# Where an expert tile's gated rows are transposed: between the two chunks of the running down product

## The reference

```
combine = jnp.sum(jax.nn.one_hot(expert_id, N_EXPERTS, dtype=f32) * w2[..., None], axis=1)
out = jnp.zeros_like(t)
for e in range(N_EXPERTS):                     # 16 experts, each token goes to 2
    hid = jax.nn.silu(t @ w_gate[e]) * (t @ w_up[e])     # 1024 -> 512
    out = out + combine[:, e:e + 1] * (hid @ w_down[e])  # 512 -> 1024
```

## Time and profile before

| | |
|---|---|
| time, median of 3 runs | 1016.9 us (1015.62 to 1018.69) |
| profiled execution | 1016.17 us, span 1014.4 us |
| PE busy | 963.5 us, 95% of the span |
| DVE busy | 670.7 us, 66% |
| ACT busy | 549.9 us, 54% |
| POOL busy | 267.7 us, 26% |
| mean granted TensorE clock | 0.988 |

### The profile page before, as it was taken

One profiled execution on the slowest core, in us unless ns is written; L12 is line 12 of the kernel. 1 busy time (PEld: TensorE's weight loads), 2 busy tenths in 40 slices (PEclk: granted clock), 3 DMA queues, 4 the chain that ended last, 5 costly groups with the idle time before them and its releaser, 6 DMA issues.

```text
span 1014.4 us, 16745 instructions
## 1 busy us (share of the span) xinstructions
PE 963.5 (95%) x5977; PEld 848.4 (84%) x5977; DVE 670.7 (66%) x860; ACT 549.9 (54%) x613; POOL 267.7 (26%) x184
## 2 busy tenths in 40 slices
PE   5999899999999999899999999989899999999986
PEld 3999789889978988799999986777688888888874
DVE  5496769669857875611111115389989899898966
ACT  5645544825544473233333214357687777878743
POOL 1014213313413231244333433015101101010161
PEclk9999999999999999999999999989899999999998
DMA  9552141304223311232332279269999999999987
GB/s 283 193 181 63 48 125 46 107 21 145 63 67 104 82 42 42 64 84 83 92 95 83 83 196 360 104 210 336 404 400 415 412 415 410 413 412 414 382 212 177
DMA packets 147847, 199.46 MB, mean 197 GB/s; under 512 B 14568, under 2 KB 91774, under 8 KB 147300
## 3 DMA queue, kind: packets, MB, share of 16 engines
q1 hardware_dynamic: 139866, 171.83, 48.9%
q0 software_dynamic: 4656, 16.21, 5.2%
q10 hardware_dynamic: 3290, 10.97, 2.8%
HBM read 176.06 MB, written 22.92 MB: 196 GB/s over the span
## 4 chain that ended last, share of the span: by engine, by line
PE 75%; DVE 14%; issue 5%; ACT 3%; DMA 1%; DVEq 1%; POOL 0%; SPq 0%; ACTq 0%
PE PJ L481 62%; DVE MEM_R L2121 3%; DVE MEM L1850 2%; PE NM L1396 2%; PE PJ L1332 2%; DVE MEM L1953 1%; PE MS L1365 1%; PE MS L1618 1%; PE NM L1553 1%; DMA MEM<-in_x_prompt_dram 1%; PE MS L1388 1%; PE PJ L1431 1%; PE NM L1654 1%; DVE M_Y L1960 1%; DMA RAW<-in_w_out_dram 1%
## 5 line engine op out<-in xcount | busy, mean ns | idle before, releaser
L481 PE MATMUL PJ<-MEM_R 128*128 128x272 f32 (+2 forms) x5016 | 799.5, 320 | 10.7 <-DVE MEM_R L2037 2.8
L481 PEld LDWEIGHTS PJ<-MEM_R 128*128 128x128 f32 x5016 | 718.2, 189 | 73.8 <-issue 12.4
L726 POOL TENSOR_TENSOR MEM_R<-RAW,MEM_R 128x1024 fp32r<-128x1024 f32 x72 | 177.6, 2474 | 343.6 <-ACT MEM_R L875 343.6
L2121 DVE TENSOR_TENSOR MEM_R<-CHUNK,MEM_R 128x2048 fp32r<-128x2048 f32 x100 | 225.5, 2294 | 16.9 <-ACT MEM_R L1138 15.7
L1138 ACT CAST MEM_R<-CHUNK 128x2048 fp32r<-128x2048 f32 x100 | 189.4, 1912 | 15.6 <-PE PJ L481 9.0
L875 ACT CAST MEM_R<-RAW 128x1024 fp32r<-128x1024 f32 x81 | 84.2, 1048 | 122.1 <-DMA RAW<-in_w_pb_dram 39.6
L2023 DVE TENSOR_TENSOR MERGED<-PJ,MEM 128x544 f32<-128x544 f32 x14 | 10.1, 725 | 132.4 <-PE PJ L481 132.4
L806 POOL COPY MEM<-MEM 128x1 uint32 (+1 forms) x16 | 22.5, 1407 | 227.0 <-PE MS L1618 227.0
L1850 DVE SCALAR_TENSOR_TENSOR MEM<-MEM 128x548 f32<-128x548 f32 x72 | 58.9, 818 | 8.5 <-DVE MEM L1848 0.9
L1156 ACT CAST MEM_R<-MS 128x1024 fp32r<-128x1024 f32 x17 | 17.3, 1017 | 27.5 <-PE MS L1618 27.5
L932 ACT COPY MEM<-PJ 128x272 f32<-128x272 f32 x24 | 9.0, 376 | 39.9 <-PE PJ L481 39.9
(11 more groups left out here) (344 smaller groups left out, 939.9 us busy)
## 6 DMA issues: line engine op xcount, KB each, us to landing
CHUNK<-in_w_gate_dram SPq DMA_DIRECT2D x34, 1024.0 KB, 7.5
CHUNK<-in_w_up_dram SPq DMA_DIRECT2D x34, 1024.0 KB, 9.2
CHUNK<-in_w_down_dram SPq DMA_DIRECT2D x34, 1024.0 KB, 8.3
RAW<-in_w_in_dram SPq DMA_DIRECT2D x56, 512.0 KB, 3.7
expert_rows<-MEM ACTq DMA_DIRECT2D x15, 512.0 KB, 6.0
expert_rows<-MEM SPq DMA_DIRECT2D x10, 512.0 KB
RAW<-in_w_pa_dram SPq DMA_DIRECT2D x8, 512.0 KB, 3.6
RAW<-in_w_pb_dram SPq DMA_DIRECT2D x8, 512.0 KB, 3.7
```

Source lines behind the costliest of these rows:

```text
L481: ins = pe.matmul(out, w(a), x(b), start=first and n == 0, stop=last and n == 2)
L726: tt(lo, raw[slot], hi.bitcast(F32), ALU.subtract).then_inc(lo_done, 1)
L2121: tt(moe_hl[c][1], moe_raw[c], moe_hl[c][0].bitcast(F32), ALU.subtract).then_inc(chunk_lo[c], 1)
```

## The change

Inside the loop and in the written-out stage ahead of it (tile 1) `down` is called in two halves, with `turn_hidden` between them. ACT's, DVE's, POOL's and SP's instructions stay as they are, and so do all matmuls and their operands.

```
             pe.wait_ge(extra_ready, 1)
-            down(1)
+            down(1, (4,))
             turn_hidden(1)
+            down(1, (5,))
             last = pe.value_load(last_i[0:1, 0:1], min_val=NE - 1, max_val=TILES - 1)
             with pe.Fori(2, TILES) as i:
                 with pe.If(i < last):
                     gate_up(i)
                     turn_rows(i + 2)
-                    down(i)
+                    down(i, (4,))
                     turn_hidden(i)
+                    down(i, (5,))
```

## The result

The changed kernel takes 1025.42 us in the median (1024.33 to 1026.72) beside 1017.8 of the kernel before: a ratio of 1.0084, with a 95% interval of 1.0062 to 1.0105. That is 7.6 us slower where 5.1 were forecast. The time lies in the stated range and the direction is right; the size is half again what was forecast. Two later comparisons of the same kernel gave 1.0061 (1.0040 to 1.0081) and 1.0078 (1.0048 to 1.0107).

A forecast was written before the change was run, and what follows sets the result against it. PE's own work was taken to bound the loop, 17.80 us a pass without waits. Terms: 3.2 (tiles 1 and 2) + 2.3 (tiles 3 to 15) − 0.4 (exit) = +5.1 us, forecast 1022.0, range 1018.2 to 1026.0.

The forecast's parts named there:

- the ring: Tiles 3 to 15: PE, ACT, DVE and back to PE takes longer than PE's own pass; 0.18 a pass, 2.3 us.
- a gain of 1.2 us by the clock at tile 1: Behind tile 1's wait: 1.6 us lost by the clock, where the kernel before lost 2.83.
- Tile 1, the wait: Ahead of tile 1's transposes: 12 matmuls move behind the wait for DVE; PE's idle 2.43 grows to 5.2 us.
- H(1): End of DVE's `hidden(1)`, tile 1's gated rows, for which its transposes wait; put at 713.59, not moved by the change.
- Tile 2: PE stalls a second time, by 2.1 us; DVE's gated rows end 16.5 us after tile 1's last down matmul.
- E(2): PE's last matmul of `down(2)`, for which ACT's result waits; put at 738.7, against 735.5 in the kernel before.
- One expected sign: In the loop: the chain of waits goes through ACT and DVE instead of PE alone, transposes 17.9 to 18.1 us apart.
- The exit: Behind the loop: its last transposes no longer stand in front of PE's 2.65 us gap, −0.4 us; clock left as traced.
- A: Only the loop's head costs, DVE in time from tile 3 on: 1019.7, or 1018.1 with short clock loss; chance 0.18.
- B: The second stall, at tile 2, lowers the clock too, 1.6 to 2.8 us more: 1023.6 to 1024.8; chance 0.17.
- C: At tiles 1 and 2 the clock gives back more than the wait takes, so faster: 1013.9; chance 0.04.
- D: No effect at all, since something else releases the transposes: 1016.9; chance 0.03.

The follow-up runs named there:

- e4: The changed kernel with DVE's gated rows put ahead of the remainder of chunk 2 in every stage: 1017.52 us, ratio 1.0005 to the kernel before.
- e13: The changed kernel with unused matmuls filling PE's idle time, 8 ahead of tile 0's transposes and 16 ahead of tile 1's: 1022.34 us, ratio 1.0057.
- e14: The kernel before with unused matmuls, 8 ahead of tile 0's transposes and 6 ahead of tile 1's: 1016.24 us, ratio 0.9996.
- e6: The kernel before with only the loop changed, transposes behind 18 of the 24 down matmuls: 1017.61 us, ratio 1.0012.
- e7: The kernel before with only the loop changed, transposes behind 6 of the 24 down matmuls: 1045.61 us, ratio 1.029.
- e1: The changed kernel measured once more, unaltered: 1022.41 us beside 1016.87 of the kernel before, ratio 1.0061.
- e2: The kernel before with only the written-out stage of tile 1 changed, the loop as before: 1018.63 us, ratio 1.0018.
- e11: The changed kernel measured a third time, unaltered: 1025.94 us beside 1018.04 of the kernel before, ratio 1.0078.
- e3: The kernel before with only the loop changed, tile 1 as before: 1019.93 us, ratio 1.0028.
- e5: The kernel before with DVE's gated rows ahead of chunk 2's remainder in every stage, at tile 1 also the gathered rows' remainder: 1016.78 us, ratio 1.0011.
- e9: As e5, with DVE's five small operations of the slot places moved behind the loop: 1017.12 us, ratio 1.0003 to the kernel before.
- e15: As e9, but the five slot-place operations run on POOL ahead of its loop: 1013.87 us, ratio 0.9979 to the kernel before.

## What held in the forecast, and which term failed

*Direction and mechanism: right.* The two waits, the ring and their causes are where the text put them, and taking away DVE's lateness (e4) takes away the cost. The step that failed is a term of the sum: a gain of 1.2 us by the clock at tile 1, where the profiles give a loss of 0.6.

*Tile 1, the wait.* The 12 matmuls went behind it. The gap became 4.32 instead of 5.2 (and 1.5 us in three profiles with the old head, not 2.43). The forecast's 5.2 holds on its own premise, full clock behind tile 0: e13 has 5.28. What differs is PE, not DVE: in the profile after, the clock fell behind tile 0, and `down(1)` began 15.23 us behind tile 0's transposes (709.24 − 694.01) instead of 13.81, while H(1) came only 0.5 later behind them (715.86 − 694.01 against 712.91 − 691.58). The length of the gap itself costs nothing: what counts is the work behind it.

*Tile 2.* 16.5 us of lag foreseen, 16.4 measured; a stall of 2.1 foreseen, 1.82 measured. From tile 1's transposes to E(2), clock kept up, e13 took 4.2 us longer than e14 (738.87 + 0.42 + 3.03 − 719.05 = 23.27 against 737.21 + 0.16 − 718.34 = 19.03). My sum without its clock terms had 4.4.

*The ring.* 0.13 a pass instead of 0.18, against the old order's 17.80; 13 passes make 1.7 instead of 2.3, and 1.4 between e13 and e14, in which the old order had one pass of 18.05. The transposes cost 0.41 to 0.42 to the next matmul, between the 0.35 and the 0.50 of the forecast. One expected sign was missing: the chain of the changed kernel's loop consists of PE (matmuls of line 481 for 92.9%, 800 to 860 us). The rows of PE's matmuls show no wait at these stalls of 0.1 us; in its first profile one of 0.36 to 0.45 stands ahead of the transposes' weight loads only.

*The exit.* −0.4 was foreseen, 0 to +0.1 came: PE idles 3.17 us there, not 2.65, and from E(15) to the next matmul it had been 3.08. In e4, with the same order but without the stalls of the ring, it idles 2.57. Yet the stalls are not what makes the gap longer: e6, whose loop has none from tile 3 on, idles 3.24, and e7, with a wait of 1.3 in each pass, 2.11. The cause stays open.

*The sum of the waits:* 6.3 forecast (5.1 with the −1.2 of the clock left out), 5.7 from the rows (4.2 + 1.4 + 0.1), 6.1 in time (e13 against e14, with some 2 us of uncertainty and the exit's clock in it).

*The term that failed is the clock's at tile 1.* I had entered 1.6 us of loss behind the new wait, the size of the loss at the loop's exit, against the 2.83 of the one profile of the kernel before, a gain of 1.2. The four profiles with the new order and an open gap (the first, e1, e2, e11) lost 2.19, 1.09, 1.12 and 1.09 on their 60 matmuls and 0.36 on the transposes (0.77 instead of 0.41 to the next matmul), 1.7 in the mean. Four with the old order there and an open gap (before, e3, e6, e7) lost 2.83, 1.6, 0 and 0, that is 1.1. So the 1.6 was about right, and the 2.83, read from a single execution, was the number that was wrong: the change loses some 0.6 us more by the clock at this place, instead of 1.2 less, 1.8 of the sum. Four profiles of each, of which two old ones lost nothing, carry these means with an uncertainty about as large as the 0.6. The clock at the exit, left as traced in the forecast, may add another 0.6. 5.7 of waits with these two terms give 6.3 to 6.9, inside the intervals of all three comparisons (6.3 to 10.7, 4.1 to 8.2, 4.9 to 10.9 us), though at the lower edge of the first; that its 7.6 lies above is put down to the scatter of four executions and not shown.

*The rivals.* A (no ring) is refuted by 17.94 and by e7; B did not happen: behind the second wait of 1.8 us 60 matmuls took 13.90 to 13.95 in all five profiles that have it. That I had ruled it out was luck, though. The row on which I did, tile 0's 2.39 without a fall, was the exception among fourteen, and behind e5's wait of 2.16, as long as the 2.1 that I had foreseen, the clock did fall. C fell with the lag of 16.4 us, D with the waits for DVE.

## What to carry to other kernels

Before a step is moved ahead of work on the engine that bounds, add up the ring: from the event that the last matmul behind it signals, through every engine in its order, back to what the moved step waits for. If that is less than what is left of the pass, nothing changes (18 matmuls ahead: 17.77); if it is a tenth of a microsecond more, it is paid in each pass. And a wait taken away at the head of such a loop comes back at the next late operand (e5) or at a queue that the moved work belonged to (e9), until its last consumer is followed as well (e15).

A loss by the clock is not to be read from one profile, not even its sign: take it from several, or keep the clock up in both kernels and compare those.

## What the runs showed of the hardware

The time of one and the same program scattered by 8 us (1011.9 to 1020.3), and the mean granted clock with it: executions of the kernel before at 0.993 took 1012.2 to 1014.8, those at 0.986 1016.3 to 1020.2. Behind the same 2.4 us of idle time PE ran on at full clock in one profile (the 48 matmuls in 11.22) and at half clock for a part in thirteen (12.1 to 12.8). Six to sixteen matmuls put into a gap took the half clock away in each of the six profiles that had them. They made the stretch behind a gap repeatable, and the kernel not measurably faster: 0.9996 and 0.9992 for the kernel before, both with 1 inside their intervals. Half clock behind the exit's gap came in 4 of 10 profiles with an idle time of 2.56 to 2.66 us, in 6 of 7 with 3.12 to 3.24, and in the one with 2.11.
